# Token-major gate and branch projections in a two-block kernel, with the merged sum transposed on the chip

## The reference

```python
u = rmsnorm(h, norm_mix_g)
p = u @ w_in + b_in                  # 1024 x 7424
aq, ak, av, hq, hf, hi, hg, gate_a, gate_b = split_columns(p)
y_attn = sliding_window_sink_attention(aq, ak, av, sinks)
y_hgrn = hgrn2_branch(hq, hf, hi, hg, lb, norm_g)
ya, yb = y_attn @ w_branch_attn, y_hgrn @ w_branch_hgrn
merged = sigmoid(gate_a) * ya + sigmoid(gate_b) * yb
h = h + merged @ w_out
# in hgrn2_branch, o being the recurrence's output, 8 heads of 128:
o = o * rsqrt(mean(o * o, -1) + EPS)          # per head
o = (o * norm_g) * sigmoid(hg)
```

## Time and profile before

| | us |
|---|---|
| median of 3 runs (794.81 to 796.19) | 795.48 |
| the profiled execution | 795.22 |
| its span, first to last instruction | 793.5 |
| TensorE busy | 780.7 |
| VectorE busy | 598.9 |
| ScalarE busy | 490.6 |

### The profile page before, as it was taken

The page is one execution under the profiler, slowest core; times in us unless marked ns, Lnnn a source line. Parts: engine busy times, 40 slices in busy tenths (PEclk is TensorE's granted clock), DMA queues, the critical chain, the costliest instruction groups (busy, mean ns, idle before and its releaser), DMA issues. The chain is left out here.

```text
span 793.5 us, 13421 instructions
## 1 busy us (share of the span) xinstructions
PE 780.7 (98%) x5512; PEld 711.0 (90%) x5512; DVE 598.9 (75%) x803; ACT 490.6 (62%) x747; POOL 18.0 (2%) x38
## 2 busy tenths in 40 slices
PE   8999999999999999999999999999999999999996
PEld 7989979999999888888888888999789999999885
DVE  5576786667876868787869897997968787777464
ACT  6878889467743564444434357866758767666441
POOL 3000001000200000000000000001000000000000
PEclk9999999999999999999999999999999999999999
DMA  8873634456444558799779993734363756545611
GB/s 303 292 266 108 212 128 140 161 190 234 161 159 160 171 202 264 245 307 318 270 265 315 349 369 117 256 110 157 107 212 97 249 165 208 161 167 178 238 54 53
DMA packets 105532, 161.01 MB, mean 203 GB/s; under 512 B 4464, under 2 KB 51712, under 8 KB 105472
## 3 DMA queue, kind: packets, MB, share of 16 engines
q1 hardware_dynamic: 105328, 159.91, 59.3%
q10 hardware_dynamic: 144, 0.26, 0.1%
HBM read 159.10 MB, written 1.06 MB: 202 GB/s over the span
## 5 line engine op out<-in xcount | busy, mean ns | idle before, releaser
L1131 DVE TENSOR_TENSOR wL<-raw,wH 128x2048 fp32r<-128x2048 f32 (+2 forms) x142 | 284.4, 2008 | 88.0 <-ACT wH L719 83.5
L1802 PE MATMUL ps<-p1H,wH 128*128 128x256 f32 x976 | 279.1, 287 | 1.8 <-DVE arena L1131 0.8
L1802 PE MATMUL ps<-p1H,wL 128*128 128x256 f32 x976 | 275.5, 283 | 0.0
L1802 PE MATMUL ps<-p1L,wH 128*128 128x256 f32 x976 | 274.1, 283 | 0.0
L719 ACT ACTIVATE wH<-raw 128x2048 fp32r<-128x2048 f32 (+1 forms) x114 | 211.9, 1863 | 83.8 <-PE ps L1805 41.8
L1802 PEld LDWEIGHTS ps<-p1H,wH 128*128 128x128 f32 x976 | 187.0, 192 | 6.6 <-issue 2.6
L1802 PEld LDWEIGHTS ps<-p1H,wL 128*128 128x128 f32 x976 | 187.1, 192 | 0.0
L1802 PEld LDWEIGHTS ps<-p1L,wH 128*128 128x128 f32 x976 | 186.3, 192 | 0.1
L1805 PE MATMUL ps<-wH,p1H 128*128 128x512 f32 x220 | 86.9, 395 | 0.0
L1805 PE MATMUL ps<-wL,p1H 128*128 128x512 f32 x220 | 85.8, 390 | 0.0
L1805 PE MATMUL ps<-wH,p1L 128*128 128x512 f32 x220 | 85.7, 390 | 0.0
(11 more groups left out here) (307 smaller groups left out, 1018.3 us busy)
## 6 DMA issues: line engine op xcount, KB each, us to landing
raw<-in_w_in SPq DMA_DIRECT2D x37, 1024.0 KB, 5.0
raw<-in_w_ada SPq DMA_DIRECT2D x24, 1024.0 KB, 5.5
raw<-in_w_up SPq DMA_DIRECT2D x44, 512.0 KB, 4.6
raw<-in_w_ffn_gate SPq DMA_DIRECT2D x22, 512.0 KB, 4.2
raw<-in_w_ffn_up SPq DMA_DIRECT2D x22, 512.0 KB, 5.4
raw<-in_w_ffn_down SPq DMA_DIRECT2D x10, 1024.0 KB, 6.7
raw<-in_w_down SPq DMA_DIRECT2D x10, 1024.0 KB, 5.1
raw<-in_w_out SPq DMA_DIRECT2D x8, 1024.0 KB, 5.0
```

The lines of the kernel that those rows point to most:

```text
L1131: return v.tensor_tensor(o, a, b, op)
L1802: last = mm(ps[:, t[1], 0:T], wt[:, slot, k, t[2]:t[2] + P], at_[:, k0 + k, :], start=st, stop=en)
```

## The change

ga, gb, hg, ba and bh become `tm` groups in two banks each, in turn 0, 1 and 2, 3; hq1's four tiles take the banks in another order. Their bias is added by VectorE from a 512-wide half of `brow`, which SyncE fills anew for each group (`B_ROWS`: six further broadcasts, each ahead of a weight load); ScalarE's sigmoid then works in place in SBUF, two instructions a group, each behind VectorE's add. The gate hG is applied in hC, token-major, by four operations a token block; hD multiplies by norm_g alone. The merged sum is token-major too, so TensorE transposes it (`merge_turn`: 16 transposes in two blocks, one inside bh1's last panel, one behind out0's first), and `merge` reads PSUM. out0 and out1 are interleaved as bh0 and bh1 are. hprep(1, 3) comes ahead of hg1's evacuation, squares(1) and merge(0) ahead of those of out1 and bh1; v_turn comes behind `scale` of unit 0.

```diff
-def cm_tiles(bank=0):
-    return [("cm", bank + m, m * P) for m in range(4)]
+def cm_tiles(bank=0, first=0):
+    return [("cm", bank + (first + m) % 4, m * P) for m in range(4)]
...
-    for _name, _c in (("q", 0), ("hq", 1280), ("hf", 2304), ("hg", 4352), ("ga", 5376), ("gb", 6400)):
-        GROUPS[f"{_name}{_i}"] = group("w_in", [(_c + _i * W, W)], cm_tiles(4 * _i if _name in ("q", "hf", "hg") else 0), "AAAA", "P1")
-    GROUPS[f"hi{_i}"] = group("w_in", [(3328 + _i * W, W)], tm_tiles(0, W, 2 - 2 * _i), "DD", "P1")
-    GROUPS[f"ba{_i}"] = group("w_branch_attn", [(_i * W, W)], cm_tiles(), "DDDD", "PY")
-    GROUPS[f"bh{_i}"] = group("w_branch_hgrn", [(_i * W, W)], cm_tiles(4 * _i), "DDDD", "PY")
+    for _name, _c in (("q", 0), ("hq", 1280), ("hf", 2304)):
+        GROUPS[f"{_name}{_i}"] = group("w_in", [(_c + _i * W, W)],
+                                    cm_tiles(4 * _i if _name in ("q", "hf") else 0, 2 * _i if _name == "hq" else 0), "AAAA", "P1")
+    for _name, _c, _b in (("hi", 3328, 2 - 2 * _i), ("hg", 4352, 2 * _i), ("ga", 5376, 2 * _i), ("gb", 6400, 2 - 2 * _i)):
+        GROUPS[f"{_name}{_i}"] = group("w_in", [(_c + _i * W, W)], tm_tiles(0, W, _b), "DD", "P1")
+    GROUPS[f"ba{_i}"] = group("w_branch_attn", [(_i * W, W)], tm_tiles(0, W, 2 * _i), "DD", "PY")
+    GROUPS[f"bh{_i}"] = group("w_branch_hgrn", [(_i * W, W)], tm_tiles(0, W, 2 * _i), "DD", "PY")
...
+B_ROWS = {"ga0": (0, 5376), "hi0": (0, 3328), "hg0": (0, 4352), "gb0": (0, 6400), "gb1": (0, 6400 + W),
+          "ga1": (1, 5376 + W), "hi1": (1, 3328 + W), "hg1": (1, 4352 + W)}
...
-    before_evac = {"oo1": [("squares", 3)], "xs": [("dt",)], "bc": [("xdt",)]}
+    before_evac = {"hg1": [("hprep", 1, 3)], "out1": [("squares", 1)], "bh1": [("merge", 0)], "oo1": [("squares", 3)], "xs": [("dt",)], "bc": [("xdt",)]}
...
-    gemm("kv", [], first[:1] + [("v_turn",)] + first[1:])
+    gemm("kv", [], first[:-1] + [("v_turn",)] + first[-1:])
...
-    gemm("hg1", [("hprep", 1, 2)], [("hprep", 1, 3)])
+    gemm("hg1", [("hprep", 1, 2)])
     gemm("ba0", [("hA", 1)], [("hB", 1)])
     gemm("ba1", [("hsplit", 0), ("hC", 1)], [("hD", 1)])
     gemm("bh0", [("hsplit", 1)], only=0)
     gemm("bh1", only=0)
-    gemm("bh0", [], [("merge", 0)], only=1)
-    gemm("bh1", [], [("merge", 1)], only=1)
-    gemm("out0")
-    gemm("out1", [("squares", 1)], [("norm", 1)])
+    gemm("bh0", only=1)
+    gemm("bh1", only=1)
+    gemm("out0", [("merge_turn", 1)], only=0)
+    gemm("out1", [("merge", 1)], only=0)
+    gemm("out0", only=1)
+    gemm("out1", [], [("norm", 1)], only=1)
...
+                    if name[:2] in ("ga", "gb", "hg"):
+                        ev["A"] += 1
+                        SIGMOID[name, m] = (on.evac_act, ev["A"])
...
-        GA, GB = scr(22, KD, T), scr(30, KD, T)
+        GA, GB = scr(22, TB, D), scr(30, TB, D)
...
-        HALVES = {"out1": EV["bh1", 2], "down1": (on.tmp_done, 16), "oo1": (on.pt_done, 9), "dd1": EV["u9", 2]}
+        HALVES = {"out1": (on.merged, 8), "down1": (on.tmp_done, 16), "oo1": (on.pt_done, 9), "dd1": EV["u9", 2]}
...
+        def merged_psum(k):
+            return ps[:, 4 + k % 4, wide(k // 4)]
...
+        rows_at = {}
+        for half_ in range(2):
+            names = [x for x in B_ROWS if B_ROWS[x][0] == half_]
+            for before_, name in zip(names, names[1:]):
+                i = next(i for i in range(NRAW, len(stream)) if taken.get(i - NRAW, -1) > at_event["evac", before_])
+                rows_at.setdefault(i, []).append((before_, name))
+        def rows(name):
+            half_, c = B_ROWS[name]
+            return brow[:, half_ * W:half_ * W + W], IN["b_in"][0:1, c:c + W].partition_broadcast(P)
...
+                for before_, name in rows_at.get(i, ()):
+                    sp.wait_ge(*EV[before_, 1])
+                    sp.dma_start(*rows(name)).then_inc(ROWS_IN[name][0], 16)
...
-                elif g in ("ga", "gb"):
-                    b0, G = (42, GA) if g == "ga" else (50, GB)
-                    each(lambda m: G[:, 4 * i + m], ACT.Sigmoid, bias=lambda m: pc("b_in", b0 + 4 * i + m))
+                elif g in ("ga", "gb", "hg"):
+                    for j in range(TB):
+                        act.wait_ge(*EV[name, j])
+                        G = hG[:, j] if g == "hg" else (GA if g == "ga" else GB)[:, j, half(i)]
+                        nc.scalar.activation(G, G, ACT.Sigmoid).then_inc(on.evac_act, 1)
...
-                        act.wait_ge(on.mixed, kk + 1)
-                        nc.scalar.activation(p1H[:, kk], GA[:, kk], ACT.Copy).then_inc(on.mh, 1)
+                        act.wait_ge(on.merge_psum, kk + 1)
+                        nc.scalar.activation(p1H[:, kk], merged_psum(kk), ACT.Copy).then_inc(on.mh, 1)
...
-                elif g == "hi":
-                    dve.wait_ge(on.in_brow, 16)
-                    if i:
+                elif g in ("hi", "hg", "ga", "gb"):
+                    dve.wait_ge(*ROWS_IN[name])
+                    if g == "hi" and i:
                         dve.wait_ge(on.o_psum, 2 * i)
                     for j in range(TB):
+                        to = {"hi": hV, "hg": hG}[g][:, j] if g[0] == "h" else (GA if g == "ga" else GB)[:, j, half(i)]
                         dve.wait_ge(on.tile_done, TILE[name, j])
-                        tt(hV[:, j], ps[:, GROUPS[name]["tiles"][j][1], :], brow[:, i * W:(i + 1) * W], ALU.add).then_inc(on.evac_dve, 1)
+                        tt(to, ps[:, GROUPS[name]["tiles"][j][1], :], rows(name)[0], ALU.add).then_inc(on.evac_dve, 1)
                 elif g == "ba":
-                    for m in range(4):
-                        dve.wait_ge(on.tile_done, TILE[name, m])
-                        tt(GA[:, 4 * i + m], ps[:, m, 0:T], GA[:, 4 * i + m], ALU.mult).then_inc(on.evac_dve, 1)
+                    for j in range(TB):
+                        a = GA[:, j, half(i)]
+                        dve.wait_ge(*SIGMOID[f"ga{i}", j])
+                        dve.wait_ge(on.tile_done, TILE[name, j])
+                        tt(a, ps[:, GROUPS[name]["tiles"][j][1], :], a, ALU.mult).then_inc(on.evac_dve, 1)
                 elif g == "bh":
-                    for m in range(4):
-                        dve.wait_ge(on.tile_done, TILE[name, m])
-                        tt(GB[:, 4 * i + m], ps[:, 4 * i + m, 0:T], GB[:, 4 * i + m], ALU.mult).then_inc(on.evac_dve, 1)
-                        dve.wait_ge(on.evac_dve, EV[name, m][1])
-                        tt(GA[:, 4 * i + m], GB[:, 4 * i + m], GA[:, 4 * i + m], ALU.add).then_inc(on.mixed, 1)
+                    for j in range(TB):
+                        a, b = GA[:, j, half(i)], GB[:, j, half(i)]
+                        dve.wait_ge(*SIGMOID[f"gb{i}", j])
+                        dve.wait_ge(on.tile_done, TILE[name, j])
+                        tt(b, ps[:, GROUPS[name]["tiles"][j][1], :], b, ALU.mult).then_inc(on.evac_dve, 1)
+                        dve.wait_ge(*EV[name, j])
+                        tt(a, b, a, ALU.add).then_inc(on.mixed, 1)
...
-                        tt(per_head(hO[:, j]), per_head(ps[:, 4 + 3 * j, :]),
-                           OR[:, j].unsqueeze(2).broadcast_to([P, 4, P]), ALU.mult).then_inc(on.o_gain, 1)
+                        dve.wait_ge(*SIGMOID[f"hg{s}", j])
+                        for h in range(4):
+                            cs = slice(h * P, h * P + P)
+                            ins = stt(hO[:, j, cs], ps[:, 4 + 3 * j, cs], OR[:, j, h:h + 1], hG[:, j, cs], ALU.mult, ALU.mult)
+                        ins.then_inc(on.o_gain, 1)
                 elif k == "hD":
                     s = e[1]
                     dve.wait_ge(on.o_bcast, s + 1)
                     for h in range(4):
-                        ins = stt(YF[s][:, h], ps[:, 5 + h // 2, wide(h % 2)], pc("hgrn_norm_g", 4 * s + h), hG[:, h],
-                                  ALU.mult, ALU.mult)
+                        ins = v.tensor_scalar(YF[s][:, h], ps[:, 5 + h // 2, wide(h % 2)], pc("hgrn_norm_g", 4 * s + h),
+                                              None, ALU.mult)
...
+            def merge_turn(i):
+                pe.wait_ge(on.mixed, 2 * i + 2)
+                pe.wait_ge(*((on.merged, 4) if i else (on.hfin, 4)))
+                for k in range(4 * i, 4 * i + 4):
+                    for j in range(TB):
+                        last = tr(merged_psum(k)[:, j * P:(j + 1) * P], GA[:, j, k * P:(k + 1) * P])
+                    last.then_inc(on.merge_psum, 1)
...
-                if (name, part) == ("bh1", 0):
-                    pe.wait_ge(on.hfin, 4)
...
-                        if (name, part, m) == ("ga0", 0, 3):
+                        if (name, part, m) == ("ga1", 0, 1):
...
+                        if (name, part, m) == ("bh1", 1, 0):
+                            merge_turn(0)
```

(37 more changed lines are left out.)

11 lines of the change are left out of this document (4 added, 7 removed).

## The result

The changed kernel took **791.40 us** (791.03 to 791.62, 4 runs) where the kernel before took 795.14 us (794.68 to 796.19) beside it: a ratio of 0.9952, with a 95% interval from 0.9940 to 0.9965. A later set of five runs of the same kernel gave 792.21 us (791.62 to 792.55), ratio 0.9960 [0.9946, 0.9974]; the median of all nine is 791.62. Forecast was 791.5, within 790.5 to 793.6.

A forecast was written before the change was run, and what follows sets the result against it. The first block was taken as bound by the number of PE instructions and their start-to-start distance. −6.1 + 1.75 + 0.27 + 0.2 = −3.9 us from the profiled 795.2 us gave a forecast of 791.5 us, range 790.5 to 793.6.

The forecast's parts named there:

- The panels: hg, ga, gb, ba, bh: 24 matmuls of 227 ns replace 48 of 120.0 in 20 panels, −6.1 us on PE.
- Rival (d): In the 20 panels the columns alone set the time, so nothing is saved: 797.7 us; chance 2%.
- The transposes: merge_turn adds 16 transposes on PE, 0.87 us for eight with the matmul behind them: +1.75 us.
- Unit 1: Attention after ga0: adds and sigmoids delay the output copy, so PE waits at unit 1's transposes, +0.27 us (0 to 0.7).
- VectorE splits a panel until E−0.25: Behind ga0: VectorE's split ends 0.25 us before E = 55.2, the end of ga0's last panel; then its adds start.
- under 0.5 us in all: Sign: PE's waits between 42 and 280 us total under 0.5 us, the only one at unit 1's transposes.
- Norm 1: squares(1) moves behind the split of out1's last panel, lengthening the serial chain to the norm's root: +0.2 us (0 to 0.5).
- Covers at nothing: Added or moved work at hC, hA(1), the bias rows before hB and the merge stays hidden from PE: no cost.
- The forecast's own sign of failure: Forecast is wrong if a bias row is what ends VectorE's idle time ahead of a gate add.
- rival (c): Bias rows land in 11.5 us, making gb0's and gb1's adds late and PE wait: 801.5 us; chance 5%.
- about 4: Assumed landing time in us of a 256 KB bias row, first in SyncE's queue, hence no cost.
- rival (a): Sigmoid's table load falls behind its wait; unit 1 pays 1.27 us, unit 2 about 0.6: 793.4 us; chance 8%.

The follow-up runs named there:

- half_width: Changed kernel with each 512-column matmul of the 20 branch and gate panels issued as two of 256 columns: 796.57 us, stretch +4.97.
- turn_twice: Changed kernel with each of the merged sum's 16 transposes issued twice: 793.68 us, stretch +1.72.
- v_turn_back: Changed kernel with the turn of the values back right behind unit 0's scores: 791.65 us, stretch −0.30.
- ada_moved: Changed kernel with the modulation panel behind ga0's first panel taken out, later ones moved up, the free place behind bh0's first panel: 790.92 us, stretch −0.71.
- squares_back: Changed kernel with the squares of out0's half ahead of the split at out1's second panel instead of behind it: 792.87 us.
- row_late: Changed kernel with gb0's bias row requested one stream panel later in SyncE's queue: 793.99 us, stretch +2.00.
- sig_late: Changed kernel with ga0's two sigmoids moved on ScalarE from ahead of unit 0's value copy to behind unit 1's turned-probability copies: 792.77 us, stretch +0.95.

## Why the prediction was right

By its own steps, for the stretch:

- **The panels.** Forecast −6.1 (0.305 each). half_width gives 5.80 us back, 0.29 a panel. The size was 5% too high: the windows it was taken from the earlier trace rows lay in runs of equal panels, while a panel between other work pays more at its ends in the 512-column form (gb1's first: 5.65 us is 0.21 above 24 x 226.7 ns; in half_width 5.93 us is 0.17 above 48 x 120.0 ns). Rival (d), that columns alone set the time, is gone. By the formula of the Trainium skill's page "TensorE: Matmul & The Clock Gate", section "Back-to-back issue gap", the saving would have been a fifth of it; the trace and this run decide against that.
- **The transposes.** Forecast +1.75 for 16. In the trace 0.79 us for eight and 0.09 at the next matmul, +1.76; sixteen more of them (turn_twice) cost 1.72.
- **Unit 1.** Forecast +0.27, bounds 0 to 0.7. Measured 0.92 (0.86 and 0.06 in front): **the one term that was mis-sized, outside its bounds.** The step that failed is "VectorE splits a panel until E−0.25". The end of ga0, E, came 0.8 us earlier than before (55.2 to 54.41) by two short panels and the start; VectorE's split ended at 55.04, E+0.6, because its own queue (the copy for the turned values, 0.42 us, now in it behind unit 0; four modulation products, 3.11; the split, 2.29) has no slack and does not come earlier with PE. The copy of attention's output, forecast at E+1.87 (0.17 late), started at E+2.4. v_turn_back gives 0.3 of it, ada_moved 0.7, and half_width, where the panels are as long as before, 0.83. With it the forecast's sign "under 0.5 us in all" failed too: the view has 0.6, the pitch 0.92.
- **The sum of the stretch.** −5.80 + 1.76 + 0.92 = −3.12; measured −3.13. Forecast for the same three terms was −4.08, so the forecast of the stretch was 0.95 us too good.
- **Norm 1.** Forecast +0.2 for the moved squares (bounds 0 to 0.5); measured +0.02. The reason given was wrong: squares_back shows that the move saves 1.1 us there. I had costed the squares by themselves and not the split that they are exchanged with.
- **Covers at nothing.** hC, hA(1), hB and the merge made no wait, as forecast. hC's products cost VectorE 0.87 us more a step (2.16 for 1.29), near the 1.0 forecast; hD's form, which the forecast took for cheaper, is not (1.66 us for four before and after). Two of the covers are now measured: hC has 1.7 and 1.4 us left; hB has 2.1 us, not the 3 of the forecast, since ScalarE's copies behind the sigmoids and not VectorE are last. The forecast's own sign of failure, a bias row that ends VectorE's idle time ahead of a gate add, did come (1.4 us at gb0) and cost nothing. The landing times of the earlier trace rows behind that term and behind rival (c) were misread: they are two requests, of which only the bias row at the start (11.5 us) is a broadcast; the 7.3 is the gate bias, a plain load at 273.5 us. The forecast's own "about 4" was near the 4.4 to 5.1 measured. Rival (c) was sound as a mechanism: row_late makes the row 3.4 us later against PE, and 2.0 of the 3.1 us go. The interleaved order was costed at nothing; as a cover it is worth 2.2.
- **The table load** ran ahead of the wait, against rival (a).
- **The total.** Forecast −3.9 from the profiled execution; its span went down 3.6. Unit 1 and the panels together cost 0.95 us more than forecast; the norm, the start and the rest gave back some 0.7, of which the start's 0.27 is chance and the rest's 0.2 was in no term. The errors nearly cancel, so that the median lies within 0.1 us of the forecast is in part luck; the direction, the mechanism and the two large terms are not.

## What to carry to other kernels

Where TensorE has no gap, count its instructions: halving their number at the same columns paid 0.29 us per panel of 48. But an engine that becomes earlier finds the others where they were: for each stretch shortened, ask which queue beside it is full, and subtract its lateness. And what is moved in a queue must be costed with what it changes places with, above all a weight split, and with the table load that it brings, as sig_late (+0.95 us) and squares_back (+1.1 us) show.

## What the runs showed of the hardware that was not expected

- Two matmuls of 256 columns, each with its weight load, take 240.0 ns and one of 512 takes 226.7 in the middle of a run (227.7 with the run's ends), both at a granted clock of 1.00: some 13 ns of each are not paid by the column. It is so too where both matmuls of a pair have the same stationary tile, loaded twice (half_width, 5.93 us for 48).
- How long a broadcast bias row takes from issue to landing went by when it was issued: at the start 11.5 us for 512 KB (before) and 9.7 and 10.7 for 256 KB each (after), singly between weight panels 4.4 to 5.1 for 256 KB (six, gb0's 4.7).
- A table load of ScalarE runs ahead of its instruction's wait (52.04, then 2.35 us of wait) and then costs nothing; with no wait behind it (sig_late, 65.04) its 1.28 us are paid in full.
- The length of the stretch between two points of PE's timeline repeated to 0.02 us (241.86, 241.88) while medians of the same kernel differed by 0.8 us: for edits of tenths it is the better measure.
